# Gate panel and branch panel of a merge tile multiplied side by side in two PSUM banks

## The reference, cut to what matters

```python
# first block: oa and hb are the two branches, [512, 1024] each
ya = oa @ w_out_a
yb = hb @ w_out_b
u = jax.nn.sigmoid(ga) * ya + jax.nn.sigmoid(gb) * yb
return x + u @ w_o
# second block
branch_a = jnp.matmul(ret.astype(dt), p_ret[l]).astype(jnp.float32)
branch_b = jnp.matmul(sb.astype(dt), p_sb[l]).astype(jnp.float32)
merged = jax.nn.sigmoid(gate_a) * branch_a + jax.nn.sigmoid(gate_b) * branch_b
x = x + jnp.matmul(merged.astype(dt), w_out[l]).astype(dt)
```

## Time and profile before

| what | value |
|---|---|
| runs, median (lowest to highest) | 3581.71 us (3575.68 to 3582.65) |
| the profiled execution: its span | 3574.0 us |
| TensorE (PE) busy | 3432.2 us, 96% of the span |
| GpSimd (POOL) busy | 1816.5 us, 51% |
| VectorE (DVE) busy | 1428.6 us, 40% |
| ScalarE (ACT) busy | 874.9 us, 24% |
| mean granted TensorE clock | 0.961 |

### The profile page before, as it was taken

One profiled execution on the slowest core, in us unless ns is written; L12 is line 12 of the kernel. 1 busy time (PEld: TensorE's weight loads), 2 busy tenths in 40 slices (PEclk: granted clock), 3 DMA queues, 4 the chain that ended last, 5 costly groups with the idle time before them and its releaser, 6 DMA issues.

```text
span 3574.0 us, 47328 instructions
## 1 busy us (share of the span) xinstructions
PE 3432.2 (96%) x15744; PEld 2803.2 (78%) x15744; DVE 1428.6 (40%) x2115; ACT 874.9 (24%) x1813; POOL 1816.5 (51%) x1028
## 2 busy tenths in 40 slices
PE   6999999998999899999999999999999999999998
PEld 4777788886777788887877788788878877878887
DVE  6666554114666554212555511201045554122021
ACT  3444333003444333002222200201132221012020
POOL 3333354663333354665444466566644445665664
PEclk9888899998888899999999999999999999999999
DMA  2222122222221121222222222222222222222222
GB/s 93 68 65 65 54 76 69 95 96 67 68 68 65 54 76 65 98 96 89 77 79 73 76 94 100 82 100 94 97 78 78 76 73 79 94 94 91 97 94 100
DMA packets 87976, 290.63 MB, mean 81 GB/s; under 512 B 12832, under 2 KB 13536, under 8 KB 87920
## 3 DMA queue, kind: packets, MB, share of 16 engines
q1 hardware_dynamic: 75024, 273.25, 22.7%
q10 hardware_dynamic: 12896, 16.64, 1.8%
HBM read 275.13 MB, written 2.10 MB: 78 GB/s over the span
## 4 chain that ended last, share of the span: by engine, by line
PE 83%; DVE 10%; issue 3%; ACT 2%; ACTq 1%; DMA 1%; DVEq 0%
PE bank L555 27%; PE bank L557 25%; PE bank L556 25%; DVE sp_lo L1352 1%; DVE xq L1418 1%; ACTq L1033 1%; PE bank L623 1%; DVE sw_hi L1351 1%; PE bank L739 1%; DVE k_hi L1351 1%; PE bank L604 1%; DMA rrq<-rq 1%; PE bank L651 1%; DVE rrq L1413 1%; DVE xk L1418 1%
## 5 line engine op out<-in xcount | busy, mean ns | idle before, releaser
L536 POOL TENSOR_SCALAR w_hi<-raw 128x1024 fp32r<-128x1024 f32 x512 | 559.4, 1093 | 1691.3 <-DMA raw<-in_w_in 1220.2
L539 POOL TENSOR_TENSOR w_lo<-raw,w_hi 128x1024 fp32r<-128x1024 f32 x512 | 1257.0, 2455 | 42.7
L555 PE MATMUL bank<-h_lo,w_hi 128*128 128x512 f32 x2816 | 1134.5, 403 | 0.7 <-issue 0.2
L556 PE MATMUL bank<-h_hi,w_lo 128*128 128x512 f32 x2816 | 1113.6, 395 | 0.0
L557 PE MATMUL bank<-h_hi,w_hi 128*128 128x512 f32 x2816 | 1112.9, 395 | 0.0
L557 PEld LDWEIGHTS bank<-h_hi,w_hi 128*128 128x128 f32 x2816 | 538.8, 191 | 116.0
L555 PEld LDWEIGHTS bank<-h_lo,w_hi 128*128 128x128 f32 x2816 | 541.8, 192 | 110.4 <-issue 2.3
L556 PEld LDWEIGHTS bank<-h_hi,w_lo 128*128 128x128 f32 x2816 | 540.8, 192 | 108.4
L1377 DVE TENSOR_TENSOR x<-x,bank 128x512 f32 x64 | 44.0, 687 | 458.3 <-PE bank L557 458.3
L556 PE MATMUL bank<-w_hi,up_lo 128*128 128x512 f32 x512 | 199.2, 389 | 0.0
L555 PE MATMUL bank<-w_lo,up_hi 128*128 128x512 f32 x512 | 199.2, 389 | 0.0
(11 more groups left out here) (309 smaller groups left out, 4843.3 us busy)
## 6 DMA issues: line engine op xcount, KB each, us to landing
raw<-in_w_in SPq DMA_DIRECT2D x288, 512.0 KB, 3.3
raw<-in_w_up SPq DMA_DIRECT2D x64, 512.0 KB, 3.2
raw<-in_w_down SPq DMA_DIRECT2D x64, 512.0 KB, 3.2
raw<-in_w_out_a SPq DMA_DIRECT2D x16, 512.0 KB, 3.2
raw<-in_w_out_b SPq DMA_DIRECT2D x16, 512.0 KB, 3.2
raw<-in_w_o SPq DMA_DIRECT2D x16, 512.0 KB, 3.3
raw<-in_p_ret SPq DMA_DIRECT2D x16, 512.0 KB, 3.2
raw<-in_p_sb SPq DMA_DIRECT2D x16, 512.0 KB, 3.2
```

Source lines behind the costliest of these rows:

```text
L536: nc.gpsimd.tensor_scalar(m.w_hi[:, slot], m.raw[:, slot], 1.0, 0.0, ALU.mult, ALU.add).then_inc(s["w_step"], 1)
L539: nc.gpsimd.tensor_tensor(m.w_lo[:, slot], m.raw[:, slot], m.w_hi[:, slot].bitcast(F32), ALU.subtract).then_inc(s["split"], 1)
L555: nc.tensor.matmul(dst, hi, rhs_lo, start=first, stop=False, **more)
L556: nc.tensor.matmul(dst, lo, rhs_hi, start=False, stop=False, **more)
```

## The change

A tile's gate panel and branch panel become a pair. The new `gemm_pair` waits until both panels are split, then runs over the 8 input tiles and in each alternates between the two banks: gate, branch, gate, branch, gate, branch. So 48 matmuls go out in which each writes another bank than the one before. The number of matmuls, their shapes and the order of the panels on SP and POOL stay as they are. The pair of branch a uses banks 0 and 1, the pair of branch b uses banks 6 and 7, and these two pairs take turns. The two `used` signals of a pair come from its last two matmuls. Banks 6 and 7 are handed over by a new semaphore, `pair_free`. Since bank 7 is `misc`, the merge begins with `misc_bank()`, and `branch_a` is now waited for ahead of the first pair. ScalarE and VectorE do the same operations as before with other banks and counts.

```diff
+            def gemm_pair(gate, branch, x_hi, x_lo):
+
+                one, two = at.slot(RING), (at.slot(RING) + 1) % RING
+                pe.wait_ge(s["split"], at.at("panel", 2))
+                for k in range(KT):
+                    w = slice(k * P, k * P + P)
+                    first, last = k == 0, k == KT - 1
+                    nc.tensor.matmul(gate[:], m.w_hi[:, one, w], m.h_lo[:, k], start=first, stop=False)
+                    nc.tensor.matmul(branch[:], m.w_hi[:, two, w], x_lo[:, k], start=first, stop=False)
+                    nc.tensor.matmul(gate[:], m.w_lo[:, one, w], m.h_hi[:, k], start=False, stop=False)
+                    nc.tensor.matmul(branch[:], m.w_lo[:, two, w], x_hi[:, k], start=False, stop=False)
+                    mm_gate = nc.tensor.matmul(gate[:], m.w_hi[:, one, w], m.h_hi[:, k], start=False, stop=last)
+                    mm = nc.tensor.matmul(branch[:], m.w_hi[:, two, w], x_hi[:, k], start=False, stop=last)
+                mm_gate.then_inc(s["used"], 1)
+                mm.then_inc(s["used"], 1)
+                at.add("panel", 2)
+
             def merge():
-                with at.loop(KT, panel=4, acc=4):
-                    h_gemm()
+                misc_bank()
+                pe.sem_inc(s["pe_step"], 1)
+                with at.loop(KT, panel=4, acc=2, u=1):
                     pe.wait_ge(s["branch_a"], at.at("merge", 1, times=KT))
-                    gemm(m.a_hi, m.a_lo)
-                    h_gemm()
+                    for c in range(2):
+                        pe.wait_ge(acc_free[c], at.at("acc", 2, div=2))
+                    gemm_pair(acc[0], acc[1], m.a_hi, m.a_lo)
+                    at.add("acc", 2)
                     pe.wait_ge(s["branch_b"], at.at("merge", 1, times=KT))
-                    gemm(m.b_hi, m.b_lo)
+                    pe.wait_ge(s["pair_free"], at.at("u", 1, times=2))
+                    gemm_pair(m.bank[6], misc, m.b_hi, m.b_lo)
+                    at.add("u")
                 at.add("merge")
...
-                with at.loop(KT, panel=4, acc=4, u=1, own=2):
+                with at.loop(KT, panel=4, acc=2, u=1, own=2):
                     act.wait_ge(s["u_ready"], at.at("u", 1))
                     sigmoid_out(m.sig_a, s["sA_ready"], free=True)
                     skip_panel()
-                    sigmoid_out(m.sig_b, s["sB_ready"], free=True)
-                    skip_panel()
+                    act.wait_ge(s["used"], at.at("panel", RING + 1))
+                    at.add("panel")
+                    own(activation(m.sig_b[:], m.bank[6][:], ACT.Sigmoid))
+                    act.sem_inc(s["pair_free"], 1)
+                    act.sem_inc(s["sB_ready"], 1)
+                    skip_panel(0)
                     at.add("u")
                 at.add("panel", PANELS_D)
...
-                with at.loop(KT, panel=4, acc=4, u=1, own=4) as n:
+                with at.loop(KT, panel=4, acc=2, u=1, own=4) as n:
                     dve.wait_ge(s["sA_ready"], at.at("u", 1))
                     take_panel()
                     c = panel_done()
                     own(tt(m.sig_a[:], acc[c][:], m.sig_a[:], ALU.mult))
                     dve.sem_inc(acc_free[c], 1)
                     dve.wait_ge(s["sB_ready"], at.at("u", 1))
-                    take_panel()
-                    c = panel_done()
-                    own(tt(m.sig_b[:], acc[c][:], m.sig_b[:], ALU.mult))
-                    dve.sem_inc(acc_free[c], 1)
+                    at.add("panel")
+                    dve.wait_ge(s["used"], at.at("panel", RING + 1))
+                    at.add("panel")
+                    own(tt(m.sig_b[:], misc[:], m.sig_b[:], ALU.mult))
+                    dve.sem_inc(s["pair_free"], 1)
                     own(tt(m.sig_a[:], m.sig_a[:], m.sig_b[:], ALU.add))
                     split(tile(m.u_hi, n), tile(m.u_lo, n), m.sig_a[:], s["u_ready"])
                     at.add("u")
+                dve.sem_inc(s["misc_free"], 1)
```

More of the change, by code:

```diff
@@ L406 @@
 raw_in0 raw_in1 raw_in2 raw_in3 acc_free0 acc_free1 split out_ready out_done used w_step pv_done h_ready
-misc_free xn_ready xT_done sq_ready ss_done vT_ready vT_done qk_ready scores_done a_ready p_ready turned
+misc_free xn_ready xT_done sq_ready ss_done vT_ready vT_done qk_ready scores_done pair_free a_ready p_ready turned
 v_ready aT_ready on_ready oT_done wif_ready gates_done rows_ready erow_ready pe_step rowsT_done sel_in
@@ L550, in _ @@
             pe.sem_inc(s["used"], RING)
+            pe.sem_inc(s["pair_free"], 2)
             pe.sem_inc(s["pv_done"], 1)
@@ L845, in _ @@
             pe.wait_ge(s["masks_ready"], 7)
-            with at.loop(DEPTH, panel=PANELS_L1, acc=PANELS_L1 - PANELS_D, xb=2, norm=1, layer=1, merge=1,
-                         a=A_HEADS, pair=B_HEADS // 2, misc=PE_MISC_L1):
+            with at.loop(DEPTH, panel=PANELS_L1, acc=PANELS_L1 - PANELS_D - 2 * KT, xb=2, norm=1, layer=1, merge=1,
+                         a=A_HEADS, pair=B_HEADS // 2, misc=PE_MISC_L1 + 1, u=KT):
                 norm()
@@ L906, in _ @@
                 project_merged()
-            with at.loop(DEPTH, panel=PANELS_L2, acc=PANELS_L2 - PANELS_D - 2 * PANELS_DOWN, xb=6, norm=2,
-                         merge=1, r=R_HEADS, half=2, misc=PE_MISC_L2):
+            with at.loop(DEPTH, panel=PANELS_L2, acc=PANELS_L2 - PANELS_D - 2 * PANELS_DOWN - 2 * KT, xb=6, norm=2,
+                         merge=1, r=R_HEADS, half=2, misc=PE_MISC_L2 + 1, u=KT):
                 norm()
@@ L1190, in _ @@
             activation(m.cos[:], m.red2[:], ACT.Sin).then_inc(s["sin_ready"], 1)
-            with at.loop(DEPTH, panel=PANELS_L1, acc=PANELS_L1 - PANELS_D, norm=1, proj=1, layer=1, a=A_HEADS,
-                         pair=B_HEADS // 2, u=KT, own=ACT_L1) as l:
+            with at.loop(DEPTH, panel=PANELS_L1, acc=PANELS_L1 - PANELS_D - 2 * KT, norm=1, proj=1, layer=1,
+                         a=A_HEADS, pair=B_HEADS // 2, u=KT, own=ACT_L1) as l:
                 log_exp_tables()
@@ L1266, in _ @@
             act.dma_start(m.sin[:], t["rot2"][:, 1]).then_inc(s["table_in"], 16)
-            with at.loop(DEPTH, panel=PANELS_L2, acc=PANELS_L2 - PANELS_D - 2 * PANELS_DOWN, norm=2, proj=3,
+            with at.loop(DEPTH, panel=PANELS_L2, acc=PANELS_L2 - PANELS_D - 2 * PANELS_DOWN - 2 * KT, norm=2, proj=3,
                          r=R_HEADS, u=KT, up=32, own=ACT_L2) as l:
@@ L1686, in _ @@
                 ts(dst[:], m.cst[:, c:c + P], 1.0, None, ALU.mult).then_inc(s["masks_ready"], 1)
-            with at.loop(DEPTH, panel=PANELS_L1, acc=PANELS_L1 - PANELS_D, norm=1, proj4=2, layer=1, a=A_HEADS,
+            with at.loop(DEPTH, panel=PANELS_L1, acc=PANELS_L1 - PANELS_D - 2 * KT, norm=1, proj4=2, layer=1, a=A_HEADS,
                          pair=B_HEADS // 2, u=KT, own=DVE_L1):
@@ L1754, in _ @@
                 add_to_x(KT)
-            with at.loop(DEPTH, panel=PANELS_L2, acc=PANELS_L2 - PANELS_D - 2 * PANELS_DOWN, norm=2, proj4=6,
+            with at.loop(DEPTH, panel=PANELS_L2, acc=PANELS_L2 - PANELS_D - 2 * PANELS_DOWN - 2 * KT, norm=2, proj4=6,
                          r=R_HEADS, u=KT, up=32, own=DVE_L2):
```

## The result

The changed kernel takes 3604.61 us (median of 4 runs, 3602.70 to 3605.31) against 3581.49 us for the kernel before (4 runs). The ratio is 1.0071 with a 95% interval of 1.0057 to 1.0086, so it is slower by 0.7%, 20 to 31 us. The profiled execution has a span of 3603.5 us and took 3605.31 us by its own time, 1.8 more than its span. Runs of the kernel before at 3575.68 us fit its trace of 3574.0 in the same way; so most of the "7.7 us" that the prediction put around the span was spread between runs, and the traces are 29.5 us apart where the medians are 23 apart.

The account below looks back on a forecast made before the run. The prediction took TensorE's matmuls to bound the merges. Starts 6.2 + 10.9, clock 5.0 and ring 11.5 summed to 33.6 us, taking the profiled 3574.0 to 3607.6 and the median to about 3615 us, range 3590 to 3650.

Parts of the forecast that it names:

- 7.7 us: Distance from the profiled execution's 3574.0 us to the median of the runs, 3581.7, assumed to stay after the change.
- Alternating banks: In the merges, matmuls that follow each other write different banks; costed at 0, matmuls staying 0.2267 us apart.
- Starts: Merges start late: first block waits for bank 7, +6.2 us; second block waits for branch a ahead of everything, +10.9 us.
- the 0.28 of the sum: Time from a release by VectorE to TensorE's matmul, read at `a_lo`, used for the first-block merge start.
- The clock: Behind TensorE's new standstills at the merge starts, work at a lowered clock: +5.0 us (0 to 10).
- the row of the long wait: Trace row of a 7.21 us TensorE wait, followed by some 6 us of work at half speed, 3 us lost.
- The ring: Weight slots in merges come free in twos; refill 11.04 us against a pair's 10.88, 0.41 lost per tile: +11.5 us.
- The step from `split` to the train of matmuls: Last part of the weight refill, from split panel to running matmuls: 0.28 + 0.09 = 0.37 us.
- the 0.24 for a w_hi stretched by `u_lo`: Behind a branch b pair, w_hi beside VectorE's `u_lo` takes 1.30 us in place of 1.06, making the refill 0.40 late.
- no wait for POOL (the ring is quicker): Sign named against the account: TensorE never waits for GpSimd's split panels inside the merges.
- the second load: Rival, chance 0.14: two weight loads in flight share, the first lands 1.2 us late; +67 us, 3649.
- this rival: Clock falls inside the merges, chance 0.03: 3.4 us at half speed for each of 56 pairs, 95 us more, 3710.

Follow-up runs that it names:

- the alternation alone: Kernel before, with only each merge matmul's bank alternating between its accumulator and bank 6, whose half is left out of the result: ratio 1.0004, span 3572.0 us.
- the first experiment: Changed kernel with the wait for bank 7 moved from ahead of the merge to ahead of the first branch b pair: ratio 1.0068, 3597.69 us.
- keeping TensorE busy: Changed kernel with unread matmuls ahead of each merge, 14 in the first block and 31 in the second: ratio 1.0083, span 3597.1 us.
- the slower split: Six more 128 x 8 GpSimd operations per panel, in the changed kernel (ratio 1.0236) and in the kernel before (ratio 1.0016).
- the earlier release: Changed kernel with gate matmuls two input tiles ahead of the branch's, so the gate's slot is released 6 matmuls ahead: ratio 1.0080 when run again.

## Why the prediction was right

The direction and the size held: +33.6 us forecast, +29.5 in the trace, +23 between the medians, and 3604.6 in the stated range. Part of that is luck, since two terms were off in opposite directions. Term by term:

- **Alternating banks, 0:** right, by the rows of the projection, and shown by the alternation alone. That a change at every matmul might differ from one at every sixth is settled.
- **Starts, 6.2 + 10.9:** 7.2 + 11.1. The mechanism is as forecast in both blocks. In the first block each start is 0.5 later than worked out. The end of the `m_branch` multiplication lies where it was forecast, 3.27 us behind the turns (620.96 - 617.69), but from there to the first matmul it takes 621.76 - 620.96 = 0.80 us and not the 0.28 of the sum. The 0.28 was read behind a wait that had only those for one accumulator and one split panel left behind it. Here the wait for bank 7 comes first, and the loop's start and the waits of L850, L830 and for `split` are gone through behind it. At the third merge, where L850 is the late one, it is 2049.85 - 2049.40 = 0.45, and in the first experiment, with fewer waits left, 617.43 - 617.09 = 0.34. So what was sized too low is the step from release to matmul; that the waits left over make the difference fits these four places, and no run tested it alone. The wait for both accumulators was overlooked too: it was hidden by the wait for bank 7 and cost nothing, until the first experiment took that away.
- **The clock, 5.0:** 8.5, mis-sized. I took half of the row of the long wait for the long standstills (1.6; measured 2.0 and 2.2) and 0.9 for the short ones (measured 2.6 and 1.6). Halving the row's 3 us was too much. The standstills of 3.5 us cost as much as those of 7.3, and the loss goes with how long TensorE worked at 0.50 (5.7, 3.4, 4.4 and 4.7 us, of which a little under half is lost each time). The mechanism is shown by keeping TensorE busy.
- **The ring, 11.5:** 2.6, the term that was mis-sized most. The mechanism is right, as the slower split and the earlier release show. Two parts of the sum were too high. The step from `split` to the train of matmuls was taken from a place where TensorE stood still (0.28 + 0.09 = 0.37); at the latest pair shown it is 0.05 to the first matmul and 0.11 more to the second, 0.16. And the 0.24 for a w_hi stretched by `u_lo` came seldom: VectorE's chain behind a pair of branch b ends at 3.8 as forecast, but w_hi takes 1.05 beside it and, in a few pairs, up to 1.16. So that refill is 3.92 + 7.02 + 0.16 = 11.10 us and a usual one, with w_hi 3.67 behind the seam, 3.67 + 7.03 + 0.16 = 10.86, under the pair's 10.88. The sum made every tile lose 0.41; in the trace only the pairs with a late w_hi lose anything that counts (w_hi starts 3.5 to 3.9 behind the seam). The sign that I had named for it, waits of 0.2 to 0.6 us for GpSimd at every second pair, didn't come, and "no wait for POOL (the ring is quicker)", named as a sign against it, did.
- The errors of clock and ring, +3.5 and -8.9, partly cancel; the sum is better than its terms.
- **The rivals:** the second load doesn't slow the first: w_hi starts 3.67 behind the seam. The clock stays at 1.00 in the merges behind the first pair; the 3.4 us at half speed that this rival was priced with came from no row shown. What the Trainium skill tells of cycling through PSUM banks ("TensorE: Matmul & The Clock Gate", section "A second HAM failure mode: psum-queue depth-cycling") is not seen here: the matmuls at a seam between pairs came at most about 0.1 us late, and the window from 2057 to 2061, inside the merge, is busy throughout. The idle time that it tells of was thus never there, and the case neither bears it out nor speaks against it. The 11 ns between 0.2267 us and the 215.7 ns of the Trainium skill ("TensorE: Matmul & The Clock Gate", section "Wait — 56ns, not 53.3ns?") stay in both kernels; what they are is open.

## What to carry to other kernels

When two units of work are merged into one, list what each waits for: the merged unit starts when the last of all of them is there, and what used to run under a wait (here 24 matmuls of the gate) now runs behind it. Then count the ring in the new unit: four slots released one by one leave the time of three panels (16.3 us) to refill one of them; released in pairs they leave the time of one pair (10.88 us) to refill two. And before an order is changed for the sake of a hardware effect, look for a place in the trace where the effect would already show; here the projection's bank changes spoke against a gain, and the alternation alone confirmed it.

## What the runs showed of the hardware that was not expected

Behind a standstill of 3.5 us TensorE's clock was at 0.50 at once in the first merge and after 0.9 us in the second, and this cost 2.6 and 1.6 us more; a standstill of 1.26 us cost nothing (first pairs of 10.98). Useless matmuls during the wait kept the clock at 1.00. Six operations of 128 x 8 on GpSimd take 0.93 us, nearly what one of 128 x 1024 takes (1.06). And the same 0.93 us more per panel made two stretches of the second block 12 to 15 us shorter each.
